# Gated delta stage: norms as logarithms in the decays' exponents, decay rows by one product a chain, the triangular inverse over all lanes, and a new order of steps

## The reference, cut to what matters

```
proj = h @ w_in                                   # q, k, v, z of width 1024 each, beta and a of width 8
qkv = silu(causal_depthwise_conv(proj[q, k, v]))  # 4 taps along the sequence
q = q * rsqrt(sum(q * q) + 1e-6) * 128 ** -0.5    # for each of 8 heads of width 128
k = k * rsqrt(sum(k * k) + 1e-6)
beta = sigmoid(b);  g = -exp(a_log) * softplus(a + dt_bias);  g_cum = cumsum(g)   # within a chunk
decay[i, j] = exp(g_cum[i] - g_cum[j])  for j <= i
lower = strict_lower(beta[i] * (k @ k.T) * decay)
u, w = solve(lower + eye, [v * beta, k * beta * exp(g_cum)])     # a triangular system
o = (q @ k.T * decay) @ (u - w @ state) + (q * exp(g_cum)) @ state     # state is carried from chunk to chunk
out = (rmsnorm(o) * silu(z)) @ w_out
```

## Time and profile before

| | |
|---|---|
| median of 3 timed runs | 2901.94 us (2901.86 to 2904.12) |
| the profiled execution's own time | 2902.29 us |
| its span in the profile | 2900.5 us |
| TensorE busy in the span | 2853.9 us |
| the two gated delta stages in the profile | about 182 to 352 us and 1660 to 1830 us |

### The profile page before, as it was taken

How to read it: one execution, slowest core, us unless ns; L and a number is a source line. 1 busy time by engine, 2 the same in 40 slices (tenths; PEclk the granted TensorE clock), 3 DMA queues, 4 the chain that set the end, 5 groups by cost and what they waited for, 6 DMA issues and landing times.

```text
span 2900.5 us, 35959 instructions
## 1 busy us (share of the span) xinstructions
PE 2853.9 (98%) x14255; PEld 2420.2 (83%) x14255; DVE 1802.8 (62%) x2186; ACT 1570.5 (54%) x1982; POOL 468.7 (16%) x694
## 2 busy tenths in 40 slices
PE   9999999999999999999999998999999999999998
PEld 7888888888988888878888897888888888888887
DVE  6559656465666556466556497566675755775664
ACT  5447754444554454565454377544565463566462
POOL 1205512021002112041202118021000020000020
PEclk9999999999999999999999999999999999999999
DMA  8764277676557677537768653486645696645694
GB/s 276 235 192 134 78 213 238 196 240 217 175 160 239 218 222 241 181 117 224 226 207 242 199 157 117 126 245 210 195 157 176 202 281 218 197 151 174 217 276 160
DMA packets 397047, 574.90 MB, mean 198 GB/s; under 512 B 20016, under 2 KB 248624, under 8 KB 396880
## 3 DMA queue, kind: packets, MB, share of 16 engines
q1 hardware_dynamic: 372624, 508.62, 55.6%
q0 software_dynamic: 23680, 62.95, 7.1%
q10 hardware_dynamic: 576, 1.05, 0.1%
HBM read 540.03 MB, written 32.51 MB: 197 GB/s over the span
## 4 chain that ended last, share of the span: by engine, by line
PE 89%; DVE 6%; ACT 4%; issue 1%; DMA 1%; SPq 0%; POOL 0%; DVEq 0%; ACTq 0%
PE ps L428 26%; PE ps L430 26%; PE ps L429 26%; PE ps L614 2%; DVE qkv L1605 2%; DVE lo L654 1%; PE ps L501 1%; PE ps L503 1%; PE ps L502 1%; ACT hi L636 1%; ACT qkv L1397 1%; PE ps L585 1%; PE ps L601 1%; ACT sl L1397 1%; ACT sy L1397 0%
## 5 line engine op out<-in xcount | busy, mean ns | idle before, releaser
L654 DVE TENSOR_TENSOR lo<-raw,hi 128x2048 fp32r<-128x2048 f32 (+3 forms) x473 | 1053.4, 2240 | 459.5 <-ACT hi L636 459.0
L636 ACT ACTIVATE hi<-raw 128x2048 fp32r<-128x2048 f32 (+2 forms) x487 | 907.1, 1872 | 762.5 <-DMA raw<-in_ffn_w_gu 272.9
L428 PE MATMUL ps<-hi,xh 128*128 128x512 f32 (+1 forms) x2208 | 867.4, 393 | 11.3 <-DVE lo L654 7.1
L430 PE MATMUL ps<-hi,xl 128*128 128x512 f32 (+1 forms) x2208 | 860.1, 390 | 0.0
L429 PE MATMUL ps<-lo,xh 128*128 128x512 f32 (+1 forms) x2208 | 859.5, 389 | 0.0
L428 PEld LDWEIGHTS ps<-hi,xh 128*128 128x128 f32 x2208 | 415.9, 188 | 96.5 <-issue 7.1
L430 PEld LDWEIGHTS ps<-hi,xl 128*128 128x128 f32 x2208 | 415.8, 188 | 85.9
L429 PEld LDWEIGHTS ps<-lo,xh 128*128 128x128 f32 x2208 | 416.2, 189 | 83.9 <-issue 0.5
L428 PE MATMUL ps<-hi,hhh 128*128 128x512 f32 x704 | 274.6, 390 | 0.0
L430 PE MATMUL ps<-hi,hhl 128*128 128x512 f32 x704 | 274.0, 389 | 0.0
L429 PE MATMUL ps<-lo,hhh 128*128 128x512 f32 x704 | 273.9, 389 | 0.0
(11 more groups left out here) (439 smaller groups left out, 3414.7 us busy)
## 6 DMA issues: line engine op xcount, KB each, us to landing
raw<-in_ffn_w_gu SPq DMA_DIRECT2D x348, 512.0 KB, 4.8
raw<-in_ffn_w_down SPq DMA_DIRECT2D x80, 1024.0 KB, 5.2
raw<-in_w_ff SPq DMA_DIRECT2D x64, 1024.0 KB, 5.7
raw<-in_w_in SPq DMA_DIRECT2D x60, 1024.0 KB, 5.2
raw<-in_gdn_w_in SPq DMA_DIRECT2D x32, 1024.0 KB, 5.6
turned<-hhf POOLq DMA_DIRECT2D x88, 256.0 KB, 4.5
hhr<-turned POOLq DMA_DIRECT2D x352, 64.0 KB, 4.0
raw<-in_sb_w_in SPq DMA_DIRECT2D x12, 1024.0 KB, 5.1
```

What stands on the lines that cost most here:

```text
L428: e.matmul(o, a1, r1, start=kk == 0, stop=False)
L430: i = e.matmul(o, a2, r1, start=False, stop=kk == kts - 1)
L636: k.e.activation(k.m.hi[q % RING][:, 0:n], k.m.raw[q % RING][:, 0:n], ACT.Copy).then_inc(*k.up("act_piece_hi", ("hi", q)))
L654: k.e.tensor_tensor(m.lo[i][:, 0:n], m.raw[i][:, 0:n], m.hi[i][:, 0:n].bitcast(F32), ALU.subtract).then_inc(*k.up("dve_piece_lo", ("split" ...
```

## The change

- The sum of squares is no longer made for every channel column. ScalarE squares all eight heads at once (2048 columns), and TensorE makes sixteen narrow products, each with 128x128 squares as its stationary side and one column of ones as its moving side, so that one PSUM bank holds the sums of all heads and rows in 16 columns. ScalarE takes the logarithm of these 16 columns (`LK`, `LQ`).
- Keys and queries are not scaled. Half the logarithm of the keys' norm goes into the exponents: `RS` and `P` are the cumulative sum with the logarithms of norm and beta added. The norm of the queries is a factor `F` that enters where the output is squared and scaled.
- The decay rows: `RS` (48 columns) is turned by one product, multiplied by a mask so that each row stands once for its head, split into two rounded parts (`ghot`), and each chain's four decay rows are then one product of 48 lanes and 512 columns with a selecting column (`gsel`).
- Beta is in the exponent too, so that `L` is one multiplication over 512 columns instead of four.
- The inverse: ScalarE writes each diagonal block twice, so that both halves of the lanes hold it; GpSimd computes the even columns on one half and the odd columns on the other, in 31 steps on about half as many columns. VectorE puts the halves together with two multiplications by a mask, a transposition and an addition.
- The scripts of all four engines are new. The logarithm of beta, the two exponentials `EK` and `BE`, and the scaling by `F` are small instructions of 8 to 16 columns.

```
@@ -34,7 +34,10 @@
 C_INV = C_ROPE + 2 * 48
 C_RST = C_INV + 16
 C_EPS = C_RST + 256
-N_CONST = C_EPS + 4
+C_SEL = C_EPS + 4
+C_MSK = C_SEL + 4
+C_HALF = C_MSK + 4
+N_CONST = C_HALF + 2
 
...
     c[:, C_EPS + 2] = -0.5 * np.log(P)
+    c[:, C_HALF:C_HALF + 2] = p % 32 // 16 == np.arange(2)[None, :]
+    r = np.arange(4)[None, :]
+    c[:, C_SEL:C_SEL + 4] = (p % 32 // 4 == r) & (p % 32 < 16)
+    c[:, C_MSK:C_MSK + 4] = p % 4 == r
...
 GDN_PE = """
-x1 W W W rbc rbc W W W W gates W W W W gates gates gates gates c1 W c3 nk nk nk c2 nk W c0 nk c2 c0 W W c3 c1 W W W W
-W W W kT W nq nq W nq W kT W W nq nq W qk W W qk rows rows W rows W qk rows c2 c0 W c1 c0 c3 c2 c0 W c0 c2 c1 a0 c3 c1
...
+x1 W W W rbc rbc W W W W gates W W W W W gates W nk nk c2 c3 c1 c0 c0 c3 W W W c2 kT c1 W kT W W W W W W W W W W qk nq
...
-SQ_BEFORE = {7: 4, 0: 6, 1: 7, 2: 5, 3: 0}
...
-def gdn_norms(silu, mean, root, sums, scaled, hps):
...
+        e.matmul(b.ps[:, 0:16], C(C_UT), r["G"].rearrange("p a b -> p (a b)"), start=True, stop=True)
+        e.matmul(b.ps[:, 16:24], C(C_ONE), r["G"][:, 0, :], start=True, stop=True).then_inc(*k.up("pe_four", ("gcum", g)))
         k.close(b)
-        for _ in range(3):
-            yield
-
-    def sums(hp):
-        b = k.take("norm", g, hp)
+        yield
+
+    def sums(a0):
+        b = k.take("sum", g, a0)
         k.wait_ge(*b.before)
-        k.wait_ge("sq", g, hp)
-        e.matmul(b.ps[:, :], C(C_ONE), r["sq"][hp % 3].rearrange("p a b -> p (a b)"), start=True, stop=True).then_inc(*k.up("pe_four", ("norm", g, hp)))
+        k.wait_ge("sq", g, a0)
+        for t in range(2):
+            for h in range(8):
+                i = e.matmul(b.ps[:, 8 * t + h:8 * t + h + 1], r["sq"][:, h, t * P:(t + 1) * P], C(C_ONE)[:, 0:1], start=True, stop=True)
+        i.then_inc(*k.up("pe_four", ("sum", g, a0)))
         k.close(b)
+
+    def nk():
+        sums(8)
+        yield
+        b = k.take("lines", g)
+        k.wait_ge(*b.before)
+        k.wait_ge("RS", g)
+        e.transpose(b.ps[0:48, 0:P], r["RS"][:, 0:48], C(C_ID)).then_inc(*k.up("pe_four", ("lines", g)))
+        k.close(b)
+        yield
+
+    def nq():
+        sums(0)
...
-        tensor_four(k, n("decay"), lambda h: r["G"][:, t, h0 + h:h0 + h + 1].to_broadcast([P, P]), lambda h: C(C_UT), ("g", g))
-        yield
-        tensor_four(k, n("kk"), kT, kT, ("qn", g, 4 + h0 // 2), ("qn", g, 5 + h0 // 2))
+        b = k.take(*n("decay"))
+        k.wait_ge(*b.before)
+        k.wait_ge("hot", g)
+        e.matmul(b.ps[:, :], r["sel"][0:48, g4:g4 + 1].to_broadcast([48, P]), r["hot"][0:48].rearrange("p a b -> p (a b)"),
+                 start=True, stop=True).then_inc(*k.up("pe_four", n("decay")))
+        k.close(b)
+        yield
+        tensor_four(k, n("kk"), kT, kT, ("qt", g, 8))
...
-        v = qkv[:, 2 * hp:2 * hp + 2, :].rearrange("p a b -> p (a b)")
-        k.wait_ge("qt", g, 8 * (hp // 4))
-        if hp in SQ_BEFORE:
-            k.wait_ge("qn", g, SQ_BEFORE[hp])
-        act("act_norms", r["sq"][hp % 3].rearrange("p a b -> p (a b)"), v, ACT.Square, ("sq", g, hp))
-
-    def root(hp):
-        b, sq = k.bank("norm", g, hp), r["sq"][hp % 3].rearrange("p a b -> p (a b)")
-        k.wait_ge("norm", g, hp)
-        act("act_norms", sq, b.ps[:, :], ACT.Ln, ("lnorm", g, hp), b.read, bias=m.eps())
-        k.wait_ge("lnorm", g, hp)
-        act("act_norms", sq, sq, ACT.Exp, ("rnorm", g, hp), scale=-0.5, bias=m.eps(2) if hp < 4 else 0.0)
+    def squares_of(a0):
+        if not a0:
+            k.wait_ge("sum", g, 8)
+        act("act_norms", r["sq"], qkv[:, a0:a0 + 8, :], ACT.Square, ("sq", g, a0))
+
+    def logs(a0, out, event):
+        b = k.bank("sum", g, a0)
+        k.wait_ge("sum", g, a0)
+        act("act_norms", out.rearrange("p a b -> p (a b)"), b.ps[:, 0:16], ACT.Ln, event, b.read, bias=m.eps())
+
+    def nk():
+        silu(8, 16)
+        yield
+        k.wait_ge("qt", g, 8)
+        squares_of(8)
+        yield
+        logs(8, r["LK"], ("LK", g))
+        yield
+        k.wait_ge("lines.s", g)
+        act("act_norms", r["hot"][0:48], r["rows"][0:48], ACT.Copy, ("hot.h", g))
+        yield
+        k.wait_ge("RS", g)
+        act("act_norms", r["EK"].rearrange("p a b -> p (a b)"), r["RS"][:, 8:24], ACT.Exp, ("ek", g))
+        k.wait_ge("P", g)
+        act("act_norms", r["BE"], r["P"][:, 8:16], ACT.Exp, ("be", g))
+        yield
+
+    def nq():
+        silu(0, 8)
+        yield
+        k.wait_ge("qt", g, 0)
+        squares_of(0)
+        yield
+        logs(0, r["LQ"], ("LQ", g))
+        yield
+        k.wait_ge("LKQ", g)
+        act("act_norms", r["F"], r["LQ"], ACT.Exp, ("F", g), scale=-0.5, bias=m.eps(2))
...
-            act("act_chain", r["Z"][q, :, 4 * g4:4 * g4 + 4], s[0][q, :, q].rearrange("p h m -> p m h"), ACT.Copy, *([n("Z")] if a == 3 else []))
+            act("act_chain", r["Z"].rearrange("p m (u k) -> p m u k", u=2)[q, :, :, 4 * g4:4 * g4 + 4],
+                s[0][q, :, q].rearrange("p h m -> p m h").unsqueeze(2).to_broadcast([32, 32, 2, 4]), ACT.Copy, *([n("Z")] if a == 3 else []))
...
+
+    def nk():
+        up = lambda *events: k.up("dve_norms", *events)
+        LK = r["LK"].rearrange("p a b -> p (a b)")
+        k.wait_ge("LK", g)
+        k.wait_ge("base", g)
+        for c in (0, 32):
+            e.scalar_tensor_tensor(RS[:, c:c + 16], LK, 0.5, GC[:, 0:16], ALU.mult, ALU.add).then_inc(*up(*([("A", g)] if c == 0 else [])))
+        k.wait_ge("A", g)
+        for c in (16, 24):
+            e.tensor_tensor(RS[:, c:c + 8], GC[:, 16:24], A[:, 0:8], ALU.subtract).then_inc(*up(*([("RS", g)] if c == 24 else [])))
+        e.scalar_tensor_tensor(PB, LK, -0.5, r["LB"].rearrange("p a b -> p (a b)"), ALU.mult, ALU.add).then_inc(*up(("P", g)))
+        yield
+        b = k.bank("lines", g)
+        k.wait_ge("lines", g)
+        e.tensor_tensor(r["rows"][0:48], b.ps[0:48, 0:P].unsqueeze(1).to_broadcast([48, 4, P]),
+                        m.const[0:48, C_MSK:C_MSK + 4].unsqueeze(2).to_broadcast([48, 4, P]), ALU.mult).then_inc(*up(("lines.s", g), b.read))
+        yield
+        k.wait_ge("hot.h", g)
+        hot = r["hot"][32:48]
+        e.tensor_tensor(hot, r["rows"][32:48], hot.bitcast(F32), ALU.subtract).then_inc(*up(("hot", g)))
...
         k.wait_ge(*n("e1"))
-        k.wait_ge("beta", g)
-        for h in range(4):
-            e.scalar_tensor_tensor(s[0][:, h, :], b.ps[:, h * P:(h + 1) * P], B[:, t, h0 + h:h0 + h + 1], s[1][:, h, :], ALU.mult, ALU.mult).then_inc(
-                *up(*([n("L"), b.read] if h == 3 else [])))
+        e.tensor_tensor(s[0][:, :, :], q4(b), s[1][:, :, :], ALU.mult).then_inc(*up(n("L"), b.read))
...
-        k.wait_ge("z0", g)
+        Z, W = (r[n].rearrange("p a b -> p (a b)") for n in "ZW")
+        up = lambda *events: k.up("dve_inv", *events)
         for j in range(4):
             k.wait_ge("Z", g, j)
-        e.transpose(r["W"].rearrange("p a b -> p (a b)"), r["Z"].rearrange("p a b -> p (a b)")).then_inc(*k.up("dve_inv", ("W", g)))
+        e.transpose(W, Z).then_inc(*up(("W", g)))
+        yield
         k.wait_ge("W", g)
-        e.tensor_scalar(r["Z"][:, :, :], r["W"].rearrange("p j i -> p i j"), -1.0, None, ALU.mult).then_inc(*k.up("dve_inv", ("V0", g)))
-        yield
         k.wait_ge("V", g)
-        e.transpose(r["W"].rearrange("p a b -> p (a b)"), r["Z"].rearrange("p a b -> p (a b)")).then_inc(*k.up("dve_inv", ("U", g)))
+        for u in range(2):
+            e.tensor_scalar(r["Z"][:, :, u:32:2], r["V"], m.const[:, C_HALF + u:C_HALF + u + 1], None, ALU.mult).then_inc(*up(*([("spread", g)] if u else [])))
+        k.wait_ge("spread", g)
+        e.transpose(W, Z).then_inc(*up(("U2", g)))
+        k.wait_ge("U2", g)
+        e.tensor_tensor(r["W"][:, :, 0:16], r["W"][:, :, 0:16], r["W"][:, :, 16:32], ALU.add).then_inc(*up(("U", g)))
...
-        e.memset(r["Z"][:, :, 16:32], 0.0).then_inc(*k.up("pool_gdn", ("z0", g)))
+        V = r["V"].rearrange("p i c -> p (i c)")
+        e.memset(V, 0.0).then_inc(*k.up("pool_inv"))
+        k.settle("pool_inv")
+        for u in range(2):
+            e.tensor_copy(V[:, 16 * u:512:33], m.const[:, C_HALF + u:C_HALF + u + 1].to_broadcast([P, 16])).then_inc(*k.up("pool_inv", *([("eye", g)] if u else [])))
...
-        v, w = r["Z"], r["W"]
-        k.wait_ge("V0", g)
-        e.memset(v.rearrange("p i j -> p (i j)")[:, 0:1024:33], 1.0).then_inc(*up())
-        for j in range(1, 31):
-            n = 31 - j
-            t = m.junk[:, 256:256 + n * j].rearrange("p (i j) -> p i j", i=n)
+        v, w = r["V"], r["W"]
+        k.wait_ge("eye", g)
+        k.wait_ge("W", g)
+        for j in range(31):
+            n, c = 31 - j, j // 2 + 1
+            t = m.junk[:, 256:256 + n * c].rearrange("p (i j) -> p i j", i=n)
             k.settle("pool_inv")
-            e.tensor_tensor(t, w[:, j, j + 1:32].unsqueeze(2).to_broadcast([P, n, j]),
```

(5 more changed lines are left out.)

136 lines of the change are left out of this document (60 added, 76 removed).

## The result

The changed kernel takes 2908.34 us (median of 20 runs, 2905.96 to 2910.13) against 2902.32 us of the kernel before (20 runs): 1.002 of its time, 95% interval 1.0013 to 1.0026, or 6.0 us slower. The forecast was 7.4 us faster. Its profiled execution has a span of 2904.6 us.

A forecast was written before the change was run, and what follows sets the result against it. TensorE, busy 98% of the span, was taken as the bound. Per stage, -4.0 us to the turning of the values and +0.3 in the tail gave -3.7, -7.4 for two: 2894.5 us, range 2884 to 2909.

The forecast's parts named there:

- The narrow products: TensorE's sums of squares for keys and queries: 64 loads a stage at 0.112 us each, 7.2 us added.
- The chain's waits: TensorE's waits in the keys' chain, ahead of sums, turned exponents and decays: 0.9, 1.1 and 2.4 us.
- The waits for remainders: TensorE's waits for VectorE's weight-piece remainders in the first stage, 2.6 and 2.3 us, were to fall away.
- The signs named for being wrong: In the trace after: narrow products at 0.3 us or more each, PEclk under 0.96, or the transposition after 261.
- the wait for `q1`'s bank: TensorE, ready at about 257.2 for the first values' projection, gets its bank at 260.4: new wait of 3.2 us.
- TensorE's path: TensorE's own sum to the turning of the values: from 306.77 before to 302.2 to 303.9.
- new low clock ... 1.7 to 3.4: On TensorE's path, half-clock cost of 1.7 to 3.4 us behind the 3.2 us wait for the bank.
- The slower rival: Keys' chain at low clock, both groups of narrow products costing twice as much: +5.9 us a stage, 2914 us; chance 0.18.
- the main case: Whole kernel 3.7 us a stage faster: 2889 to 2899 us, point 2894.5; chance 0.42.
- the inverse's second half: VectorE's masks, transposition and addition after GpSimd's result: 2 x 0.6 + 1.25 + 0.65 us, ending at about 307.
- the transposition at 258.5: Inverse's transposition on VectorE, behind ScalarE's eight block copies at 0.45 to 0.6 us: moves from 254.59 to 258.5.
- VectorE beside GpSimd: From 259.7, seven convolution steps (five at 5.11 us, two at 3.74) and three splits at 2.65: 41.0 us, to 300.7.

The follow-up runs named there:

- e1: Changed kernel with filling products on TensorE in the three waits of the keys' chain; 2906.6 us.
- e3_pool_later: Changed kernel with GpSimd's splits waiting for the end of the inverse's second half on VectorE in place of the last convolution; 2900.6 us.
- e4_bank: Changed kernel with only the second query convolution moved ahead of the inverse's transposition (VectorE) and the last chain's block copies (ScalarE); 2895.3 us.
- e7_pool_bank: Changed kernel with the edits of e3_pool_later and e4_bank together: GpSimd's splits later, second query convolution sooner; 2894.7 us.
- e10_pool_bank_128: e7_pool_bank with each narrow product of the norms made on up to 128 columns of ones in place of one; 2896.5 us.
- e12: e4_bank with narrow products on up to 128 columns of ones and filling products in the keys' chain; 2890.2 us.
- e8: e3_pool_later with the narrow products of the norms made on 32 columns of ones in place of one; 2898.9 us.
- e11: e10_pool_bank_128 with filling products on TensorE in the waits of the keys' chain; 2892.6 us.

## Why the prediction was wrong

**Right.** The narrow products: 32 records in 3.63 us at full clock (at 293.32), 0.113 each, where 0.112 was taken. The chain's waits: 0.73, 0.85 and 2.24 us for 0.9, 1.1 and 2.4. The waits for remainders went. The decays ran as rounded products (2.04 us at half clock, 1.18 at full in e1). The work fell by 2.7 to 2.9 us for 2.4, when the low clock is priced by the spacing of the products. The signs named for being wrong did appear: PEclk was 0.93 and 0.94, under 0.96, and the transposition came at 263.18, after 261.

**Right by luck: the wait for `q1`'s bank.** It was 2.94 us (3.57 in the second stage) for 3.2. But TensorE came to it at 262.1 in place of 257.2 and the bank was read at 265.0 in place of 260.4; two errors of the same size cancelled.

The turning of the values parts the loss. Lengths in us, first / second stage; low clock is half of the busy time at 0.50 up to the turning:

| | start to turning | idle in it | low clock in it | turning to output |
|---|---|---|---|---|
| before | 124.8 / 125.3 | 9.0 / 10.3 | 3.4 / 2.6 | 45.4 / 45.4 |
| forecast, from before | -4.0 | -0.5 | -1.7 to 0 | +0.3 |
| after | 125.5 / 125.9 | 7.6 / 8.5 | 8.7 / 8.3 | 48.7 / 47.1 |
| e3_pool_later | 126.2 / 124.5 | 8.3 / 8.2 | 8.7 / 7.0 | 43.8 / 43.8 |
| e4_bank | 122.3 / 123.0 | 5.9 / 6.6 | 7.0 / 7.0 | 44.8 / 43.8 |
| e7_pool_bank | 122.7 / 123.1 | 6.4 / 6.7 | 7.0 / 7.0 | 43.8 / 43.8 |
| e10_pool_bank_128 | 118.0 / 119.0 | 6.5 / 6.3 | 1.7 / 2.9 | 48.5 / 48.6 |

Of the 13.6 us a run between forecast and result, 9.3 lie ahead of the turning and the rest behind it.

**Wrong, first: TensorE's path, in its term "new low clock ... 1.7 to 3.4".** The low clock cost 8.7 and 8.3 us up to the turning, some 5.3 of the first in the keys' chain, and so TensorE was at the values at 307.61 in place of 302.2 to 303.9. Work and idle time up to there came out a little better than forecast; the gain of 4.0 us was lost to the clock. e10 against e7 shows it by one edit: with the low clock down by 5.3 and 4.1 us the values are turned 4.7 and 4.2 us sooner. The slower rival named the place and the cause, with 0.18; its 2914 was 5.7 us too high, where the main case was 13.8 too low. The forecast's own argument against it, the full clock of 128-column products in the stage before, did not carry over to products of one column.

**Wrong, second: the inverse's second half, "2 x 0.6 + 1.25 + 0.65".** It took 6.13 + 1.25 + 3.70 and a little between, 11.1 us in place of 3.1. I had used the rows on VectorE and GpSimd for GpSimd's side alone, the operation of 2.48 us beside a split, and not for VectorE's side, although GpSimd's splits begin with the last convolution and so lie on just these instructions. The before-trace could not warn: there only a transposition stood in that place. e3 shows the cause and its price, 7.8 us for the kernel, all of it behind the turning.

**Wrong, third: the transposition at 258.5.** It came at 263.18. The eight copies of two chains took 0.68 each (5.43 us) where 0.45 to 0.6 was taken, and VectorE waited 1.54 and 1.39 us for products and exponentials in the chain. VectorE stood idle for 3.04 us ahead of it, which the forecast's row of additions had not looked for. The order that left this idle time beside the wait for `q1`'s bank is the dearest choice of the change: undoing it is worth 13.0 us (e4). It isn't an error of the sum, though, which had the wait at its measured price; and the 13.0 us hold a good part of the second error's price too.

**VectorE beside GpSimd** was less disturbed than taken: seven convolution steps and three splits in 38.6 us from the transposition's end for 41.0, a convolution's multiplication at 580 ns on average for 735.

A fuller clock is won back as time only when nothing else is late. e10's 4.7 and 4.2 us went into a wait for GpSimd's split and the low clock around it. e12 against e4 is 5.1 us (4.3 when each is set against its own runs of the kernel before), for 7.0 and 5.3 us of low clock saved, with 4.6 to 5.0 us a stage of filling and wider products added on TensorE. It is not settled by these runs why narrow products of one or 32 columns go with the low clock more than those of 128 do, and how much of the 10.4 us would be won with everything else in time.

## What to carry to other kernels

When a change halves the work on GpSimd, look at what VectorE does when GpSimd turns to its next job: the collision moves, and an instruction of 0.4 us can take 3. Ahead of a long instruction that waits for another engine's copies, put the independent work whose first step frees a bank. Where TensorE's own path is level with another engine's, price the low clock behind every group of thin products and every wait in a forecast. But check what arrives last at the end of the stage, because a fuller clock can be given back as a wait a few products later.

## What the runs showed of the hardware

- Sixteen 32-bit products (32 records) cost 3.63 us with one moving column and 3.73 with up to 128 (e10, 287.65 us of its span): each record brings its own weight load, and columns up to 128 are nearly free. At 0.50 both kinds cost 0.213 us a record. The queries' group has no idle time ahead in the changed kernel, e3 and e8, and in all three (one column, one, 32) a stretch at 0.50 begins within or right behind it; in e10 (128 columns) none of the four groups has one, though 1.5 and 1.6 us of idle time lie ahead of the queries', where in e7, with one column and 1.6 us, both have. With 128 columns and 1.8 to 2.1 us of idle time ahead, a stretch at 0.50 begins within the group in four cases (three in e11, one in e12) and not in a fifth (e12, 286.51, 2.02 us).
- A multiplication of 128x512 from SBUF to SBUF on VectorE took 0.44 us alone (two in 0.87, e3) and 3.1 us (two in 6.13) beside a GpSimd subtraction over 2048 columns. That itself took 6.60 us in place of 4.63, with VectorE's own split of 2048 columns beside its first 2.1 us; the split took its usual 2.28. Beside such a subtraction a transposition of 1024 columns took 1.25 us and a multiplication that reads PSUM 0.68, as without it (L1766 at 311.89 and L1751 at 305.12 after the change; L1718 at 307.13 and L1706 at 308.30 before).
